# Gate and up products of the dense feed-forward networks with high and low rows side by side

## What is computed

```python
def swiglu(x, w_gate, w_up, w_down):          # x 256 x 1024, w_gate and w_up 1024 x 2816, w_down 2816 x 1024
    return (jax.nn.silu(x @ w_gate) * (x @ w_up)) @ w_down
```

## Time and profile before

| | |
|---|---|
| median of 3 runs | 3217.68 us (3214.59 to 3220.85) |
| profiled execution | 3202.12 us, its span 3200.2 us |
| TensorE busy | 3018.2 us, 94% |
| VectorE busy | 1887.5 us, 59% |
| ScalarE busy | 1357.2 us, 42% |
| matmuls | 15994 |
| mean granted TensorE clock | 0.978 |

### The profile page before, as it was taken

One profiled execution on the slowest core, in us unless ns is written; L12 is line 12 of the kernel. 1 busy time (PEld: TensorE's weight loads), 2 busy tenths in 40 slices (PEclk: granted clock), 3 DMA queues, 4 the chain that ended last, 5 costly groups with the idle time before them and its releaser, 6 DMA issues.

```text
span 3200.2 us, 41798 instructions
## 1 busy us (share of the span) xinstructions
PE 3018.2 (94%) x15994; PEld 2479.7 (77%) x15994; DVE 1887.5 (59%) x2376; ACT 1357.2 (42%) x1556; POOL 47.5 (1%) x93
## 2 busy tenths in 40 slices
PE   6999998999999999989999999988999999999998
PEld 6987786589899868766997599554877877787776
DVE  6654633276677283235670355153887788778877
ACT  4431211144444122222441254233666766676665
POOL 2000010000000000000000000000000000000000
PEclk9999999999899999999999999998999999999999
DMA  7754321377577333126762364322988998899886
GB/s 256 246 171 145 115 106 55 105 241 245 193 265 242 118 116 117 42 81 212 240 231 100 124 197 158 136 75 105 355 313 312 344 342 308 302 344 336 309 318 224
DMA packets 373337, 659.67 MB, mean 206 GB/s; under 512 B 9034, under 2 KB 195256, under 8 KB 373240
## 3 DMA queue, kind: packets, MB, share of 16 engines
q1 hardware_dynamic: 373240, 658.31, 58.6%
HBM read 657.23 MB, written 1.05 MB: 206 GB/s over the span
## 4 chain that ended last, share of the span: by engine, by line
PE 74%; DVE 10%; issue 5%; ACT 3%; DVEq 3%; DMA 2%; PEld 1%; PEldq 1%; ACTq 0%; SPq 0%
PE banks L649 16%; PE banks L650 16%; PE banks L651 16%; PE banks L1109 9%; PE banks L1871 3%; DVE ffn_tmp L1596 3%; PE banks L1903 2%; PE banks L645 2%; PE banks L1268 2%; DVE ffn_arena L974 1%; DVE mod_sum L967 1%; PE banks L722 1%; PE banks L808 1%; PE banks L794 1%; DVE expert_rest L1035 1%
## 5 line engine op out<-in xcount | busy, mean ns | idle before, releaser
L649 PE MATMUL banks<-ffn_arena 128*128 128x256 f32 (+1 forms) x3460 | 1169.4, 338 | 66.2 <-DVE expert_rest L1035 33.0
L651 PE MATMUL banks<-ffn_arena 128*128 128x256 f32 (+1 forms) x3460 | 1150.9, 333 | 0.0
L649 PEld LDWEIGHTS banks<-ffn_arena 128*128 128x128 f32 x3460 | 662.5, 191 | 141.2 <-issue 42.1
L1035 DVE TENSOR_TENSOR expert_rest<-expert_raw,ffn_arena 128x2048 fp32r<-128x2048 f32 (+1 forms) x306 | 648.0, 2162 | 117.3 <-ACT ffn_arena L896 112.1
L651 PEld LDWEIGHTS banks<-ffn_arena 128*128 128x128 f32 x3460 | 662.2, 191 | 69.7
L650 PE MATMUL banks<-ffn_arena 128*128 128x256 f32 (+1 forms) x2200 | 673.1, 306 | 0.0
L896 ACT ACTIVATE ffn_arena<-expert_raw 128x2048 fp32r<-128x2048 f32 (+1 forms) x306 | 538.2, 1809 | 260.2 <-PE banks L651 118.9
L650 PE MATMUL banks<-expert_rest,ffn_arena 128*128 128x512 f32 (+1 forms) x1224 | 467.3, 382 | 0.0
L650 PEld LDWEIGHTS banks<-ffn_arena 128*128 128x128 f32 x2200 | 424.2, 193 | 17.3 <-issue 0.5
L1109 PE MATMUL banks<-HT,panel 128*128 128x256 f32 x1408 | 314.4, 385 | 2.7 <-issue 2.7
L1109 PEld LDWEIGHTS banks<-HT,panel 128*128 128x128 f32 x1408 | 270.3, 193 | 42.9 <-issue 5.9
(11 more groups left out here) (396 smaller groups left out, 2738.4 us busy)
## 6 DMA issues: line engine op xcount, KB each, us to landing
expert_raw<-in_moe_w_gate_dram SPq DMA_DIRECT2D x45, 2048.0 KB, 8.1
expert_raw<-in_moe_w_up_dram SPq DMA_DIRECT2D x45, 2048.0 KB, 7.9
expert_raw<-in_moe_w_down_dram SPq DMA_DIRECT2D x45, 2048.0 KB, 7.7
gate_w<-in_ffn_w_gate_dram SPq DMA_DIRECT2D x55, 1024.0 KB, 5.4
up_w<-in_ffn_w_up_dram SPq DMA_DIRECT2D x55, 1024.0 KB, 5.4
down_w<-in_ffn_w_down_dram SPq DMA_DIRECT2D x55, 1024.0 KB, 5.4
mod_unit<-in_mod_w_dram SPq DMA_DIRECT2D x48, 1024.0 KB, 5.1
panel<-in_w_in_dram SPq DMA_DIRECT2D x24, 2048.0 KB, 8.0
```

The costliest lines, as they stand in the source:

```text
L649: mm(out, w[0], x[0], start=start, stop=False)
L651: return mm(out, w[1], x[0], start=False, stop=stop)
L1035: last = tt(rest[:, half, :], tile[:, half, :], high[:, half, :].bitcast(F32), ALU.subtract)
```

## The change

The high and the low rows of the input are laid side by side for each block k (`x_both`), and one matmul with the high weights takes both, 512 moving columns, into a whole bank; the low weights take the high rows alone, 256 columns, into the bank's first half. So a product has 32 matmuls where it had 48, and each block `f` has a bank: gate in banks 4 and 5, up in banks 6 and 7. The two halves of a bank must then be added. For the gate ScalarE copies the second halves to SBUF and VectorE adds the first halves, ahead of the Silu (now from SBUF). For the up product ScalarE copies (`up_rest_act`) and VectorE adds, then multiplies. The semaphores `silu_done` and `unit_ready` count three and two per step. The next gate product waits for all three of ScalarE's marks of the step before, the copy of the up product among them. On ScalarE that copy stands behind the high part of the next gate weights (behind that of the last down weights in step 10).

```diff
-        x_parts, unit_parts = parts(2048, 2048, KD, SEQ), parts(0, 512, FB, SEQ)
+        x_both, unit_parts = v3(ffn_arena, 2048, KD, 2, SEQ), parts(0, 512, FB, SEQ)
+        x_parts = [x_both[:, :, j, :] for j in range(2)]
...
             for f in range(FB):
                 for k in range(KD):
-                    last = split_mm(banks[:, bank, f * SEQ:(f + 1) * SEQ], [w[:, k, f * P:(f + 1) * P] for w in weights],
-                                    [v[:, k, :] for v in x_parts], k == 0, k == KD - 1)
+                    high, low = [w[:, k, f * P:(f + 1) * P] for w in weights]
+                    both = x_both[:, k, :, :].rearrange("p j c -> p (j c)")
+                    if k == 0:
+                        mm(banks[:, bank + f, :], high, both, start=True, stop=False)
+                    mm(banks[:, bank + f, 0:SEQ], low, x_parts[0][:, k, :], start=False, stop=False)
+                    if k:
+                        last = mm(banks[:, bank + f, :], high, both, start=False, stop=k == KD - 1)
             return last
 
         def ffn_gate(pe, n, s, ffn_in=ffn_in):
             pe.wait_ge(gate_low, n + s + 2)
-            pe.wait_ge(silu_done, n + s + 1)
+            pe.wait_ge(silu_done, (n + s) * 3 + 1)
             ffn_in(4, gate_parts).then_inc(gate_done, 1)
 
         def ffn_up(pe, n, s, ffn_in=ffn_in):
             pe.wait_ge(up_low, n + s + 2)
-            pe.wait_ge(unit_ready, n + s + 1)
-            ffn_in(5, up_parts).then_inc(up_done, 1)
+            pe.wait_ge(unit_ready, (n + s) * 2 + 1)
+            ffn_in(6, up_parts).then_inc(up_done, 1)
...
         def silu_act(act, n, s, width):
             act.wait_ge(gate_done, n + s + 2)
-            act.wait_ge(unit_ready, n + s + 1)
-            act_fn(ffn_tmp[:, 0:width], banks[:, 4, 0:width], ACT.Silu).then_inc(silu_done, 1)
+            act.wait_ge(unit_ready, (n + s) * 2 + 1)
+            act_fn(v3(ffn_tmp, 0, FB, SEQ), banks[:, 4:6, SEQ:], ACT.Copy).then_inc(silu_done, 1)
+            act.wait_ge(unit_ready, (n + s) * 2 + 2)
+            act_fn(ffn_tmp[:, 0:width], ffn_tmp[:, 0:width], ACT.Silu).then_inc(silu_done, 1)
+
+        def up_rest_act(act, n, s):
+            act.wait_ge(up_done, n + s + 2)
+            act.wait_ge(act_ready, n + s)
+            act_fn(act_t, banks[:, 6:8, SEQ:], ACT.Copy).then_inc(silu_done, 1)
...
                     panel_high(act, n, s, down_in, gate_done, down_w, last_down_parts, down_high)
+                    up_rest_act(act, n, s)
                 else:
                     gate_act(act, n, s + 1)
+                    up_rest_act(act, n, s)
                     up_act(act, n, s + 1)
                     down_act(act, n, s)
-                act.wait_ge(unit_ready, n + s + 2)
+                act.wait_ge(unit_ready, (n + s) * 2 + 3)
...
+        def gate_sum_vec(dve, n, s):
+            dve.wait_ge(silu_done, (n + s) * 3 + 2)
+            tt(v3(ffn_tmp, 0, FB, SEQ), v3(ffn_tmp, 0, FB, SEQ), banks[:, 4:6, 0:SEQ], ALU.add).then_inc(unit_ready, 1)
+
         def unit_vec(dve, n, s, width):
-            dve.wait_ge(silu_done, n + s + 2)
-            dve.wait_ge(up_done, n + s + 2)
-            tt(v3(ffn_tmp, FB * SEQ, width), ffn_tmp[:, 0:width], banks[:, 5, 0:width], ALU.mult).then_inc(unit_ready, 1)
+            dve.wait_ge(silu_done, (n + s) * 3 + 4)
+            tt(act_t, act_t, banks[:, 6:8, 0:SEQ], ALU.add)
+            dve.drain()
+            tt(v3(ffn_tmp, FB * SEQ, width), ffn_tmp[:, 0:width], v3(ffn_tmp, FB * SEQ, width), ALU.mult).then_inc(unit_ready, 1)
 
         def ffn_vec(dve, n, m=None):
 
             def step(s, final=False):
+                gate_sum_vec(dve, n, s)
                 if not final:
                     gate_vec(dve, n, s + 1)
```

More of the change, by code:

```diff
@@ L735, in expert_gate_pe @@
         def expert_gate_pe(pe, i, s, step):
-            pe.wait_ge(silu_done, step)
+            pe.wait_ge(silu_done, 2 * E_AT + step)
             expert_in_pe(pe, i, f"g{s}", 4)
         def expert_up_pe(pe, i, s, step):
-            pe.wait_ge(unit_ready, step)
+            pe.wait_ge(unit_ready, E_AT + step)
             expert_in_pe(pe, i, f"u{s}", 5)
         def expert_turn_pe(pe, s, step):
-            pe.wait_ge(unit_ready, step + 2)
+            pe.wait_ge(unit_ready, E_AT + step + 2)
             for f in range(expert_cols(s) // P):
@@ L899, in expert_silu_act @@
             act.wait_ge(expert_used, E_BASE + expert_done(i, f"g{s}"))
-            act.wait_ge(unit_ready, step + 1)
+            act.wait_ge(unit_ready, E_AT + step + 1)
             act_fn(ffn_tmp[:, 0:width], banks[:, 4, 0:width], ACT.Silu).then_inc(silu_done, 1)
@@ L1038, in expert_unit_vec @@
         def expert_unit_vec(dve, i, s, step, width):
-            dve.wait_ge(silu_done, step + 2)
+            dve.wait_ge(silu_done, 2 * E_AT + step + 2)
             dve.wait_ge(expert_used, E_BASE + expert_done(i, f"u{s}"))
```

## The result

| | kernel before | changed kernel |
|---|---|---|
| median | 3217.86 us (8 runs, 3211.43 to 3220.85) | 3226.85 us (8 runs, 3225.58 to 3235.27) |
| profiled execution | 3202.12 us, span 3200.2 | 3225.75 us, span 3224.0 |
| TensorE busy, matmuls | 3018.2 us, 15994 | 3021.2 us, 14234 |
| VectorE / ScalarE busy | 1887.5 / 1357.2 us | 1961.8 / 1483.7 us |
| mean granted clock | 0.978 | 0.971 |

The changed kernel takes 1.0036 times as long (95%: 1.0024 to 1.0048), 9.0 us more by the medians, where +9.9 was forecast. It has 1760 matmuls fewer and is slower all the same, by less than half a per cent.

A forecast was written before the change was run, and what follows sets the result against it. TensorE, busy 94% of the span, was taken to bound the kernel. Starts +8.1, middle −19.2, ends +16.2 and clock +4.8 gave +9.9 us, 3212.0 on the profiled execution, 3227.6 us as median; range 3213 to 3243.

The forecast's parts named there:

- Matmuls: TensorE, 18 products in each of five feed-forward networks: fewer matmuls save 0.213 us per product, −19.2 us in all.
- one 13.3 ns goes for each block: TensorE, gate and up products: 512 + 256 columns take 347 ns where three 256s take 360.
- faster rival: TensorE: the weight switch hides behind the 512, a pair costs 333 ns, total 3208.5 us; chance 0.12.
- that of no gain: TensorE: a pair costs 355 to 360 ns, the losses stay, total 3240 to 3247 us; chance 0.07.
- Table loads and the step: Middle steps, counted from T, the gate product's end: two loads of 1.29 us, Silu at 3.45; still bound by TensorE.
- rival of one load: ScalarE: one table load serves Copy and Silu, chain 1.3 us shorter, total 3218 us; chance 0.13.
- that of a second load behind the add: ScalarE: the second load waits for VectorE's add, VectorE's circle is 17.0 us, total 3252 us; chance 0.06.
- Starts: First steps of the five feed-forward networks: TensorE waits longer for ScalarE and VectorE, +8.1 us in all.
- new gap: First steps: TensorE waits 1.9 us ahead of the second gate product, for the low gate weights.
- Ends: Last steps: late last down weights and the unit product delay the last down product, +16.2 us over five feed-forward networks.
- Clock: Behind four 4.5 us TensorE waits at the ends the clock drops, 1.2 us each, +4.8 us; starts 0.
- The sum: Whole program: 8.1 − 19.2 + 16.2 + 4.8 = +9.9 us; forecast chance 0.62.

The follow-up runs named there:

- hidden loads: Changed kernel with a one-column Silu at the head of each ScalarE step, ahead of the wait for the gate product: 3216.21 us, 1.0008 of the kernel before.
- weights early: Changed kernel with the last down weights fetched early into the gate weights' buffer and VectorE's last modulation share cut in pieces: 3210.78 us, 0.9988 of the kernel before.
- idle matmuls: Changed kernel with six idle 512-column matmuls ahead of the last step's down product: 3222.20 us, 1.0020 of the kernel before.
- bank wait: Changed kernel, next gate product waiting for VectorE's gate add instead of ScalarE's up copy, except in first steps: 3226.00 us, 1.0034 of the kernel before.
- all repairs: Changed kernel with table loads ahead of the wait, modulation behind the up weights, last down weights fetched early: 3190.74 us, 0.9927 of the kernel before.

## Why the prediction was right

**Matmuls.** The mechanism held, the size was a quarter too large: 10.5 ns a pair were saved (360 against 349.5), not 13.3. The term that was mis-sized is "one 13.3 ns goes for each block": the spacings of 256 among 256 and of 512 among 512 were carried over to a place where no row had shown them. A step is 16.63 us, not 16.56. By the steps the middle is 45 × 0.353 = 15.9 us shorter, 15.1 of them in the 90 products (16 × 10.5 ns each); some 1 us of the −16.8 measured is low clock (2.9 us in before, above five middles of 152.8 us; 2.0 in after, above 149.65). Neither the faster rival (333 ns) nor that of no gain was true. The 2.5 ns a matmul of the Trainium skill ("TensorE: Matmul & The Clock Gate", "Back-to-back issue gap") would make the pair 325 ns; the measured 349.5 decides against it for this mix of widths, and the matmuls that went were dearer than that section has them. That section states it for an isolated matmul, which the prediction leaves out; for a stream of weight loads and matmuls it has 131 ns at 512 columns, and the 227 ns of rows 2 don't agree with that either.

**Table loads and the step.** Two loads in every middle step; Silu at T + 3.47 (forecast 3.45), gate weights' low half at T + 5.09 (5.03), unit product at T + 12.62 (12.67), last subtraction at T + 17.78 (17.8), 0.34 us left ahead of the next gate add (0.3). The rival of one load falls by 120.25, and with it, for this loop, the longest run of one table set by which the Trainium skill ("ScalarE activation tables: per-element evaluation and per-set limits", "Table sets in the compiler and the runtime") places loads; that of a second load behind the add falls by the same row, as it starts 0.02 us ahead of the add. The prediction's own chain had the second load end 0.58 us behind the add (3.45 against 2.87), and 0.56 us is what came out when it was taken away. The rival of one load counted 1.3 us for it all the same, so its 3218 was too low, and the expectation of the hidden loads counted 2.6 us for both, where 1.85 is right.

**Starts.** Forecast per FFN +2.2, +1.0, +2.5, +1.1, +1.3, measured +2.2, +0.7, +2.9, +2.4, +1.6. The new gap is there (1.84 us for 1.9). The fourth FFN's first gate product holds some 1.5 us at the low clock: 14.82 us to its second gate product at a granted clock of 0.88, where the same kernel run again took 13.25 us at 1.00. Without it the sum is +8.3.

**Ends.** The last step's down product starts at T + 12.8, as worked out; the weights land at T + 6.44 (worked out: 3.42 + 3.1), and their transfer, not the modulation, ended last. Sum +16.2 and +16.2. With the weights early, 9.1 us of it went.

**Clock.** The right mechanism, a size too small: 1.6 us an end, not 1.2, four times; together +6.5 for +4.8. The idle matmuls and the early weights both show it, by opposite means. For the gaps at the starts nothing was counted; behind them the changed kernel lost 1.6 us, in the first FFN (granted clock 0.72 from 49.9 to 56.0), where before had lost some 2.5 in its second and fourth together.

**The sum.** The terms' errors add up to 5.8 us, +15.7 in the FFNs for +9.9; that the medians show +9.0 (12.2 and 11.4 in the two repeats, the bank wait counted as one) makes the forecast look better than its terms were. That 9.0 lies so near 9.9 is therefore partly luck. Where the 3 to 7 us between the pieces and the medians lie isn't settled: the rest of the program varies by 11 us from one profile to the next, the kernel before has only one profile, and no run here held that still. The direction and the place of every part were as forecast.

## What to carry to other kernels

Fewer instructions of the same total columns gave 3% of each product here, and only while the work that they push to other engines stays beside TensorE: count, for every loop, the first step, the last step and the middle ones separately, as the middle ones had room for the added work and the ends had none. At the ends ask what the added work delays through the buffers (a transfer issued late, with the clock behind the wait for it, cost about what all pairs gave), and count a long wait of TensorE with the slow matmuls behind it. Where a table load stands in a chain, a tiny activation of the right kind ahead of the wait takes it out.

## What was not expected of the hardware

- 512 and 256 columns with other weights in turn take 349.5 ns a pair, 2.5 ns more than the sum of their spacings among their own kind (227 and 120).
- Of TensorE's waits at the ends, those of 2.0 and 2.39 us were followed by a clock of 1.00, those of 2.93, 3.68 and 4.36 us by matmuls 0.42 us apart (a clock near 0.50); the 36 matmuls of such a tail took 1.5 to 2.9 us longer. It isn't a matter of the wait alone: with the loads hidden, the fifth FFN lost 1.6 us behind a stop of 2.70 us from start to start, and with all repairs one of 2.89 us lost nothing.
- The chip's time outside the changed part varied by 11 us between profiles of kernels that do the same there, more than the 9 us that the change makes in the medians.
- A Copy directly ahead of a Silu at the head of a loop draws a load of 1.28 us for each of them, every time round; in the last step, which stands behind the loop, neither draws one (201.51).
